# Two of three portions of each down projection as seven block products (Strassen's scheme)

## The chip, the cores and the metric

The kernel runs on one core of a Trainium2 chip. The metric is the device time of one execution in microseconds (us), as the median of repeated runs. The profile is one execution that the hardware profiler recorded; its engines are PE (TensorE), DVE (VectorE), ACT (ScalarE), POOL (GpSimd) and SP (SyncE, which issues the DMAs).

## The reference

Three layers on 512 tokens of 1024 features in float32: a sparse attention mixer and an FFN, a retention mixer and an FFN, a gated block with three branches and an FFN. The change touches the three FFNs alone, and of them the last product. One FFN is:

```python
def conv_ffn(h, w_up, conv_w, conv_b, w_down):
    seq = h.shape[1]
    u = h @ w_up
    up = jnp.pad(u, ((0, 0), (CONV_W - 1, 0), (0, 0)))
    u = sum(up[:, j:j + seq] * conv_w[j] for j in range(CONV_W)) + conv_b
    a, b = u[..., :D_FF], u[..., D_FF:]
    return (jax.nn.silu(a) * b) @ w_down
```

and the layer adds its result to `x`.

## The kernel before

**Layout and precision.** Activations stand with features on the 128 partitions and the 512 tokens along the free dimension: `X` holds 8 feature blocks of 128x512, `H` the normalised input. Each float32 product is made of three matmuls on rounded parts (`mm3`, lines 335 to 337): weight high part by activation high part, high by low, low by high. So each weight block (128x128) is loaded three times.

**Weights.** They come in units of up to 128x1024 (8 blocks for one output feature block), in one long order. SP loads a unit by DMA into one of four raw slots (`WS`, `load_to`, line 286). ACT rounds it to its high part (`WH`, `hi_to`, line 306), POOL takes the low part (`WL`, `lo_to`, line 316), three units at a time in `WH` and `WL`. A slot of `WH` is free when PE has used the unit three before. `hi_to` is called at fixed places of ACT's program, up to a unit counted from the one whose result ACT handles there (`P.ahead`).

**One FFN** has 22 pairs of up units (`up p` and `up 22+p`, 24 matmuls of 512 columns each) and three down portions over 8, 8 and 6 of the 22 inner feature blocks (`FFN_GROUPS`), each of 8 units with one output feature block. PE's order is ups 0 to 15, down 0, ups 16 to 21, down 1, down 2 (`pe_ffn`, line 578). For each up unit DVE multiplies the sum by the norm's row (line 664, "scaling"), ACT writes the third tap of the convolution (line 622, "tap") and DVE adds the two others (lines 666, 669). Then ACT takes the silu (line 626), DVE multiplies the halves (line 674), ACT rounds the product into `G` (line 632) and DVE takes its low part (line 677). For a down unit DVE adds the result to `X` (`dve_add_x`, line 571). At the start of an FFN the first scaling has to wait for the norm's row, so DVE and ACT begin some units behind PE.

Each engine executes its own fixed program; semaphores join them. Sums stand in eight PSUM banks (`ps`) of 128x512.

Two other places serve the prediction as measures: the gtg products of the gated block (line 335 on `G`, 16 groups of three matmuls of 256 columns) and the 64-row products of its attention (line 1863).

Of the kernel before, what the change touches and what calls it, by code (L numbers as in the profile page):

```python
# [16 lines left out]
T = 512  # L17
# [4 lines left out]
FFN_GROUPS = [(0, 8), (8, 16), (16, 22)]  # L22
RING = 3
STAGE = 4
# [4 lines left out]
def weight_units():  # L29
# [120 lines left out]
class Plan:  # L150


    def __init__(self, mem, dram, counted=None, sems=None):
        self.m, self.d, self.sems = mem, dram, sems
        self.count, self.value = {}, {}
        self.known = counted.value if counted else {}
        self.places = unit_places()[0]
        self.order = counted.order if counted else []
        self.index = counted.index if counted else {}
        self.unit_end = counted.unit_end if counted else {}  # L160
# [4 lines left out]
        self.hi_n = self.lo_n = self.in_n = 0  # L165
# [111 lines left out]

def load_to(P, e, n):

    while P.in_n < min(n, len(P.order)):  # L280
        i = P.in_n
        at, w = P.places[P.order[i]]
        if i >= STAGE:
            e.wait_ge(*P.at("w_lo", i - STAGE))
# [3 lines left out]
        P.in_n += 1  # L288


def w_parts(P, i):
    w = P.places[P.order[i]][1]
    s, f = i % RING * NXW, i % STAGE * NXW
    return P.m["WH"][:, s:s + w], P.m["WL"][:, s:s + w], P.m["WS"][:, f:f + w]


def hi_to(P, e, n):

    while P.hi_n < min(n, len(P.order)):
# [4 lines left out]
        if i >= RING:  # L304
            e.wait_ge(*P.at(*P.unit_end[i - RING]))
# [13 lines left out]
def unit(P, e, key, end):  # L319

    if key not in P.index:
        P.index[key] = len(P.order)
        P.order.append(key)
    if key not in P.begun:
        P.begun.add(key)
        e.wait_ge(*P.at("w_lo", P.index[key]))
    i = P.index[key]
    P.unit_end[i] = end
    w = P.places[key][1]
    s = i % RING * NXW  # L330
    return P.m["WH"][:, s:s + w], P.m["WL"][:, s:s + w]
# [245 lines left out]

def pe_ffn(P, e, L, ph):
    def up(g):
        for p in range(*FFN_GROUPS[g]):  # L580
            for m in (p, FT + p):
                feature(P, e, ("up", L, m), P.hs(), ready=(lambda k: [("h_lo", (ph, k))]) if m == 0 else None)
                if m == FT:
                    if L == 0:
                        e.wait_ge(*P.at("cr", "mean"))
                    row_mm(P, e, ph)

    def down(g):
        a, z = FFN_GROUPS[g]
        for m in range(8):  # L590
            feature(P, e, ("dn", L, g, m), [(P.G(p % 16 * T), P.G(8192 + p % 16 * T)) for p in range(a, z)],
                    ready=(lambda n: [("g_lo", (L, a + n))]) if m == 0 else None)
    up(0)
    up(1)
    down(0)
    up(2)
    down(1)
    down(2)


def act_ffn(P, e, L, ph, after, g_end, sc_end):
# [3 lines left out]
    def up(g):  # L605
        for p in range(*FFN_GROUPS[g]):
            s = 2 * (p % 2)
            for m, slot in ((p, s), (FT + p, s + 1)):
                key = ("up", L, m)
                if p == 0 and slot == 0:  # L610
                    e.preload_act_table_set("natural_log_exp_and_others")
                    act_row_split(P, e, ph, 7)
                    hi_to(P, e, P.ahead(("up", L, FT)))
                    act_row(P, e, ph)
                    hi_to(P, e, P.ahead(("up", L, 1), True))
                    e.wait_ge(*P.at("fp", L))
                    for ev in sc_end:
                        e.wait_ge(*P.at(*ev))
                if p >= 2:
                    e.wait_ge(*P.at(*(("silu", (L, p - 2)) if slot == s else ("mul", (L, p - 2)))))  # L620
                e.wait_ge(*P.at("f_u", key))
                e.activation(P.sc(slot * T), P.ps(key), ACT.Identity, bias=fp[:, 4 * m + 3:4 * m + 4],  # L622
                             scale=fp[:, 4 * m + 2:4 * m + 3]).then_inc(*P.sig("tap2", key))
                hi_to(P, e, P.ahead(key, True) + (1 if p in (1, 2, 3) else 0))
            e.wait_ge(*P.at("conv", ("up", L, p)))
            e.activation(P.ps(("up", L, p)), P.sc(s * T), ACT.Silu).then_inc(*P.sig("silu", (L, p)))
            e.wait_ge(*P.at("mul", (L, p)))
            if p == 0 and g_end:
# [5 lines left out]
    def down(g):
        for m in range(8):
            key = ("dn", L, g, m)
            hi_to(P, e, P.ahead(key))
            if after and g == 2:
                act_x(P, e, after, m, ("x", key))
    up(0)  # L640
    up(1)
    down(0)
    up(2)
    down(1)
    down(2)


def dve_ffn(P, e, L, ph, after, sc_end):
# [6 lines left out]
    def up(g):  # L655
        for p in range(*FFN_GROUPS[g]):
            s = 2 * (p % 2)
            for m, slot in ((p, s), (FT + p, s + 1)):
                key, c = ("up", L, m), P.sc(slot * T)
                u = P.ps(key)  # L660
                e.wait_ge(*P.at("feat", key))
                if m == 0:
                    e.wait_ge(*P.at("row", ph))
                e.tensor_tensor(u, u, P.m["ACC"][:, :], ALU.mult).then_inc(*P.sig("f_u", key))  # L664
                e.wait_ge(*P.at("tap2", key))
                e.scalar_tensor_tensor(c[:, 1:T], u[:, 0:T - 1], fp[:, 4 * m + 1:4 * m + 2], c[:, 1:T], ALU.mult,  # L666
                                       ALU.add).then_inc(*P.sig("tap1", key))
                e.wait_ge(*P.at("tap1", key))
                e.scalar_tensor_tensor(c[:, 2:T], u[:, 0:T - 2], fp[:, 4 * m:4 * m + 1], c[:, 2:T], ALU.mult,  # L669
                                       ALU.add).then_inc(*P.sig("conv", key))  # L670
            gate, g = P.ps(("up", L, p)), P.ps(("up", L, FT + p))
            e.wait_ge(*P.at("silu", (L, p)))
            e.wait_ge(*P.at("conv", ("up", L, FT + p)))
            e.tensor_tensor(g, gate, P.sc((s + 1) * T), ALU.mult).then_inc(*P.sig("mul", (L, p)))
            P.end["ps", ("up", L, p)] = ("mul", (L, p))
            e.wait_ge(*P.at("g_hi", (L, p)))
            e.tensor_tensor(P.G(8192 + p % 16 * T), g, P.G(p % 16 * T).bitcast(F), ALU.subtract).then_inc(
                *P.sig("g_lo", (L, p)))
            P.end["ps", ("up", L, FT + p)] = ("g_lo", (L, p))

    def down(g):
        for m in range(8):
            dve_add_x(P, e, ("dn", L, g, m), m, ("x", ("dn", L, g - 1, m)) if g else None)
            if after and g == 2 and m:
                dve_x(P, e, after, m - 1)
        if after and g == 2:
            dve_x(P, e, after, 7)
    up(0)
    up(1)
    down(0)  # L690
    up(2)
    down(1)
    down(2)


def pool_ffn(P, e, L):
    lo_to(P, e, P.ahead(("dn", L, 2, 7)))

# [1790 lines left out]
def act_program(P, e):  # L2489
# [12 lines left out]
    act_ret(P, e, "nf1", ("feat", ("dn", 0, 2, 7)))  # L2502
# [43 lines left out]
def sp_program(P, e):  # L2546
# [19 lines left out]
    weights(("dn", 0, 2, 6))  # L2566
# [10 lines left out]
    for m in range(8):  # L2577
        e.wait_ge(*P.at("x", ("dn", 1, 2, m)))
# [100 lines left out]
```

## Time and profile before

| | |
|---|---|
| median of three runs | 2140.15 us (2139.69 to 2142.06) |
| the profiled execution | 2140.16 us |
| its span (first to last instruction) | 2138.0 us |
| PE matmuls | 9723, busy 2122.6 us |
| granted TensorE clock | 1.0 over the span |
| DMA | 200.4 MB, mean 94 GB/s |

The span is what the trace covers; the execution's own time is 2.2 us longer. PE's busy time is the union of its matmuls, each of which overlaps the next: a 512-column matmul is shown with 390 ns and the next one starts 227 ns after it. The pace is therefore read from starts, not from durations. "Idle before" of an engine is time in which it waited, with the operation that ended the wait.

### The profile page before, as it was taken

Reading aid. Unit: us, or ns where it says so; the run is one execution under the profiler, and the core shown is the slowest. Engines: PE = TensorE matmul, PEld = TensorE weight load, DVE = VectorE, ACT = ScalarE, POOL = GpSimd, SP = SyncE. Lnnn points to the kernel's source line nnn. Section 1 sums busy time; section 2 is a strip of 40 time slices with the busy share of each in tenths; the row PEclk is TensorE's granted clock in tenths of the full one; section 3 lists DMA queues with packets and bytes.
Section 4 is the critical chain, followed back from the end, with each engine's and each line's share of the span. In section 5 each row is a group of like instructions: output and inputs, shape, how many; then the busy total and the mean of one; then the engine's idle time right before and its main releaser. Section 6 shows DMA issues by size and latency. Waiting matters only on the chain.

```text
span 2138.0 us, 25128 instructions
## 1 busy us (share of the span) xinstructions
PE 2122.6 (99%) x9723; PEld 1755.1 (82%) x9723; DVE 1094.9 (51%) x1756; ACT 931.5 (44%) x1378; POOL 924.6 (43%) x428
## 2 busy tenths in 40 slices
PE   9999999999999999999999999999999999999999
PEld 7868888888888888878888888888887888888887
DVE  7973555151634445475552424997577324553331
ACT  6564444242433424354442324445877434443331
POOL 3504444444434343434444444655432554444443
PEclk9999999999999999999999999999999999999999
DMA  4203232232322222222222224322222243223222
GB/s 165 70 11 103 97 98 93 87 109 92 121 84 89 84 99 74 98 73 97 94 94 101 96 87 167 107 80 79 70 70 70 95 134 99 98 94 102 91 94 84
DMA packets 57654, 200.41 MB, mean 94 GB/s; under 512 B 6400, under 2 KB 7168, under 8 KB 57280
## 3 DMA queue, kind: packets, MB, share of 16 engines
q1 hardware_dynamic: 56816, 197.46, 27.6%
q8 instruction: 78, 1.28, 0.3%
q10 hardware_dynamic: 720, 1.34, 0.2%
q14 instruction: 40, 0.33, 0.0%
HBM read 194.32 MB, written 4.19 MB: 93 GB/s over the span
## 4 chain that ended last, share of the span: by engine, by line
PE 96%; DVE 2%; issue 1%; ACT 1%; DMA 0%; ACTq 0%; DVEq 0%; POOL 0%
PE ps L335 29%; PE ps L337 28%; PE ps L336 28%; PE ps L365 2%; PE ps L363 2%; PE ps L364 2%; PE ps L1878 1%; PE ps L1271 1%; PE ps L1863 0%; PE ps L1890 0%; DMA X<-in_x 0%; PE ps L378 0%; PE ps L1865 0%; PE ps L1887 0%; DVE SC L2331 0%
## 5 line engine op out<-in xcount | busy, mean ns | idle before, releaser
L316 POOL TENSOR_TENSOR WL<-WS,WH 128x1024 fp32r<-128x1024 f32 (+1 forms) x360 | 853.1, 2371 | 1124.9 <-ACT WH L306 1124.6
L335 PE MATMUL ps<-H,WH 128*128 128x512 f32 (+2 forms) x1776 | 693.2, 390 | 2.8 <-DVE H L543 2.0
L337 PE MATMUL ps<-H,WL 128*128 128x512 f32 (+2 forms) x1776 | 690.5, 389 | 0.0
L336 PE MATMUL ps<-H,WH 128*128 128x512 f32 (+2 forms) x1776 | 690.5, 389 | 0.0
L306 ACT ACTIVATE WH<-WS 128x1024 fp32r<-128x1024 f32 (+2 forms) x362 | 374.8, 1037 | 432.5 <-PE ps L337 352.5
L335 PEld LDWEIGHTS ps<-H,WH 128*128 128x128 f32 (+1 forms) x1776 | 333.3, 188 | 73.8 <-DVE H L543 3.7
L337 PEld LDWEIGHTS ps<-H,WL 128*128 128x128 f32 (+1 forms) x1776 | 333.1, 188 | 69.1
L336 PEld LDWEIGHTS ps<-H,WH 128*128 128x128 f32 (+1 forms) x1776 | 333.4, 188 | 66.0
L335 PE MATMUL ps<-G,WH 128*128 128x512 f32 x880 | 343.2, 390 | 2.0 <-DVE G L1597 1.4
L337 PE MATMUL ps<-G,WL 128*128 128x512 f32 x880 | 342.8, 389 | 0.0
L336 PE MATMUL ps<-G,WH 128*128 128x512 f32 x880 | 342.8, 389 | 0.0
L571 DVE TENSOR_TENSOR X<-X,ps 128x512 f32<-128x512 f32 x120 | 81.7, 686 | 339.2 <-PE ps L337 338.4
L622 ACT ACTIVATE SC<-ps,FP 128x512 f32<-128x512 f32 x132 | 102.9, 779 | 334.4 <-DVE ps L664 334.4
L335 PEld LDWEIGHTS ps<-G,WH 128*128 128x128 f32 x880 | 165.3, 188 | 37.0 <-DVE G L1597 1.8
L337 PEld LDWEIGHTS ps<-G,WL 128*128 128x128 f32 x880 | 165.3, 188 | 34.4
L336 PEld LDWEIGHTS ps<-G,WH 128*128 128x128 f32 x880 | 165.3, 188 | 33.9
L666 DVE SCALAR_TENSOR_TENSOR SC<-ps,FP,SC 128x511 f32<-128x511 f32 x132 | 99.0, 750 | 125.8 <-ACT SC L622 125.8
L664 DVE TENSOR_TENSOR ps<-ps,ACC 128x512 f32<-128x512 f32 x132 | 92.1, 697 | 134.4 <-PE ps L337 128.1
L669 DVE SCALAR_TENSOR_TENSOR SC<-ps,FP,SC 128x510 f32<-128x510 f32 x132 | 98.9, 749 | 4.7
L2185 DVE SCALAR_TENSOR_TENSOR ps<-SC,PAR,ps 128x512 f32<-128x512 f32 x116 | 82.2, 754 | 1.9
L363 PE MATMUL ps<-WH,H 128*128 128x512 f32 x192 | 75.2, 392 | 0.0
L365 PE MATMUL ps<-WH,H 128*128 128x512 f32 x192 | 74.8, 389 | 0.0
(271 smaller groups left out, 1943.6 us busy)
## 6 DMA issues: line engine op xcount, KB each, us to landing
WS<-in_w SPq DMA_DIRECT2D x337, 512.0 KB, 3.2
WS<-in_w SPq DMA_DIRECT2D x24, 384.0 KB, 3.0
xs<-X SPq DMA_DIRECT2D x1, 2048.0 KB, 6.2
X<-xs SPq DMA_DIRECT2D x8, 256.0 KB, 4.0
out<-X SPq DMA_DIRECT2D x8, 256.0 KB, 2.0
X<-in_sg SPq DMA_DIRECT2D x1, 1344.0 KB, 5.6
X<-in_x ACTq DMA_DIRECT2D x4, 256.0 KB, 6.8
X<-in_x SPq DMA_DIRECT2D x4, 256.0 KB, 6.2
```

The source lines that it names most:

```text
L306: e.activation(hi, raw, ACT.Copy).then_inc(*P.sig("w_hi", i))
L316: e.tensor_tensor(lo, raw, hi.bitcast(F), ALU.subtract).then_inc(*P.sig("w_lo", i))
L335: e.matmul(out, lh, rh, start=start, stop=False)
L336: e.matmul(out, lh, rl, start=False, stop=False)
L337: return e.matmul(out, ll, rh, start=False, stop=stop)
L363: e.matmul(o, hh, wh[:, w], start=k == 0, stop=False)
L365: t = e.matmul(o, hl, wh[:, w], start=False, stop=k == 7)
L622: e.activation(P.sc(slot * T), P.ps(key), ACT.Identity, bias=fp[:, 4 * m + 3:4 * m + 4], scale=fp[:, 4 * m + 2:4 * m + 3]).then_inc(*P.sig ...
L664: e.tensor_tensor(u, u, P.m["ACC"][:, :], ALU.mult).then_inc(*P.sig("f_u", key))
L666: e.scalar_tensor_tensor(c[:, 1:T], u[:, 0:T - 1], fp[:, 4 * m + 1:4 * m + 2], c[:, 1:T], ALU.mult, ALU.add).then_inc(*P.sig("tap1", key))
L669: e.scalar_tensor_tensor(c[:, 2:T], u[:, 0:T - 2], fp[:, 4 * m:4 * m + 1], c[:, 2:T], ALU.mult, ALU.add).then_inc(*P.sig("conv", key))
L2185: e.scalar_tensor_tensor(c if j else P.sc(k * T), p[:, j:j + T], P.par("cvw", j * 4 + k), c, ALU.mult, ALU.add).then_inc(*P.sig("tap", (k, ...
```

## The change

The first two portions of each down projection (8 inner feature blocks each) are computed by Strassen's scheme in Winograd's form. For a pair `mp` of output feature blocks (m1, m2), the weights are split by even and odd inner blocks and by m1 and m2 into a11, a21, a12, a22, each four blocks of 128x128 side by side (128x512). The activations are split by even and odd blocks and by token halves, 256 columns each. In place of eight block products there are seven: a11, s1, s2, a12, s3, s4 and a22, where s1 = a21 + a22, s2 = s1 - a11, s3 = a11 - a21, s4 = a12 - s2. Each is 4 x 3 matmuls of 256 columns into half a PSUM bank, four pairs a portion.

- **PE** (`pe_down_pair`): the products in that order. a11, s2, s3 and a22 add onto one another in bank A, s1 and s4 in bank C, a12 has bank B. Between them DVE adds the state of the bank to a quarter of the pair's X, and PE waits for that before it goes on in the bank: s2 waits for the addition after a11, s3 for that after s2, a22 for that after s3, s4 for that after s1.
- **DVE**: the four weight sums of each pair from the raw slots into PSUM (`dve_sum`), their low parts (`dve_sum_lo`), and the seven additions of 256 columns (`dve_take`), in place of two of 512.
- **ACT**: the high parts of a11, a12, a22 and of the four sums (`act_form`). **POOL**: the low parts of a11, a12, a22 (`pool_raw_lo`). `WH` and `WL` are now six cells of 512, of which a unit takes two and a product one; a cell is free when PE has used what was there six cells before.
- **Activation forms**: the seven products need seven forms of the gated products, two of them plain. ACT and DVE make them while the up units run (`forms_1`, `forms_2`), for block p within the work on block p+1.
- **Order**: ups 0 to 9, first portion, ups 10 to 21, second portion, third portion. The convolution of the last up unit before a portion is put between the additions of its last pair.
- In `act_ffn` the call of `hi_to` for the first half reads `P.ahead(key, True)`, without one more for pairs 1 to 3.

The third portion keeps its form. The core of the diff:

```diff
-FFN_GROUPS = [(0, 8), (8, 16), (16, 22)]
+FFN_UPS = [(0, 10), (10, 22)]
...
+def pe_product(P, e, pair, name, low, o, form, first):
+
+    key = (pair, name)
+    cells(P, key, 1)
+    hi, lo = P.cell(key)
+    e.wait_ge(*P.at(low, key))
+    for q in range(4):
+        w = slice(128 * q, 128 * q + 128)
+        bh, bl = P.GX(4 * pair[1] + q, form, 0), P.GX(4 * pair[1] + q, form, 1)
+        e.matmul(o, hi[:, w], bh, start=first and q == 0, stop=False, skip_group_check=True)
+        e.matmul(o, hi[:, w], bl, start=False, stop=False, skip_group_check=True)
+        t = e.matmul(o, lo[:, w], bh, start=False, stop=q == 3, skip_group_check=True)
+    t.then_inc(*P.sig("prod", key))
...
+    a = own("A", seats["A", pair[2] % 2])
+    pe_product(P, e, pair, "a11", "w_lo", a, UP_B11, True)
+    c = own("C", seats["C"])
+    pe_product(P, e, pair, "s1", "fs_lo", c, UP_T1, True)
+    e.wait_ge(*P.at("x", (pair, "a11")))
+    pe_product(P, e, pair, "s2", "fs_lo", a, UP_T2, False)
+    b = own("B", seats["B"])
+    pe_product(P, e, pair, "a12", "w_lo", b, UP_B21, True)
+    e.wait_ge(*P.at("x", (pair, "s2")))
+    pe_product(P, e, pair, "s3", "fs_lo", a, UP_T3, False)
+    e.wait_ge(*P.at("x", (pair, "s1")))
+    pe_product(P, e, pair, "s4", "fs_lo", c, UP_B22, False)
+    e.wait_ge(*P.at("x", (pair, "s3")))
+    pe_product(P, e, pair, "a22", "w_lo", a, UP_T4, False)
...
-                hi_to(P, e, P.ahead(key, True) + (1 if p in (1, 2, 3) else 0))
...
+            tap2(p, s)
+            forms_1(p - 1)
+            if p < z - 1:
+                hi_to(P, e, P.ahead(("up", L, p), True))
+            forms_2(p - 1)
+            if p < z - 1:
+                tap2(FT + p, s + 1)
+                hi_to(P, e, P.ahead(("up", L, FT + p), True))
+                silu(p)
+                product(p)
+        for name in ("s2", "a12", "s3", "s4", "a22"):
+            act_form(P, e, (L, g, 0), name)
...
+    if name == "s1":
+        t = e.tensor_tensor(o, P.raw(pair, "a21"), P.raw(pair, "a22"), ALU.add)
...
+        t = e.tensor_tensor(o, P.ps((pair, "s1")), P.raw(pair, "a11"), ALU.subtract)
...
+        t = e.tensor_tensor(o, P.raw(pair, "a11"), P.raw(pair, "a21"), ALU.subtract)
...
+        t = e.tensor_tensor(o, P.raw(pair, "a12"), P.ps((pair, "s2")), ALU.subtract)
...
+def dve_take(P, e, pair, name, bank_name, m, half, before=None):
+
+    x = P.X(2 * pair[2] + m)[:, 256 * half:256 * half + 256]
+    e.wait_ge(*P.at("prod", (pair, name)))
+    e.tensor_tensor(x, x, P.ps((pair, bank_name))[:, 0:256], ALU.add).then_inc(*P.sig("x", (pair, name)))
```

The order on ACT at the start of an FFN, from the first silu on (line 626 before, 771 now), before:

```order
L626 ACTIVATE ps<-SC 128x512
L632 ACTIVATE G<-ps 128x512
L622 ACTIVATE SC<-ps,FP 128x512
L306 ACTIVATE WH<-WS 128x1024
L622 ACTIVATE SC<-ps,FP 128x512
L306 ACTIVATE WH<-WS 128x1024
L626 ACTIVATE ps<-SC 128x512
L632 ACTIVATE G<-ps 128x512
L622 ACTIVATE SC<-ps,FP 128x512
L306 ACTIVATE WH<-WS 128x1024
```

and now (765 is the tap, 361 the cast of a weight unit, 784, 786, 797 and 800 the activation forms):

```order
L771 ACTIVATE ps<-SC 128x512
L784 ACTIVATE SC<-ps 128x512
L765 ACTIVATE SC<-ps,FP 128x512
L797 ACTIVATE G_long<-ps 128x512
L765 ACTIVATE SC<-ps,FP 128x512
L361 ACTIVATE WH<-WS 128x1024
L771 ACTIVATE ps<-SC 128x512
L786 ACTIVATE G_long<-ps 128x512
L765 ACTIVATE SC<-ps,FP 128x512
L800 ACTIVATE G_long<-ps 128x256
L361 ACTIVATE WH<-WS 128x1024
```

The first cast (unit 6) stood behind the first tap of pair 1 and now stands behind the second; the next one (unit 7) stood behind that second tap and now stands behind the silu, a form, the first tap of pair 2 and another form.

The order on DVE in one settled pair of the first portion, from the addition after a11 on (line 888 is an addition to X, 878 a low part, 861, 866, 864 and 869 the next pair's sums s1, s3, s2 and s4); before, a down unit had one addition of 512 columns on DVE and nothing else there:

```order
L888 TENSOR_TENSOR X<-X,ps 128x256
L878 TENSOR_TENSOR WL<-ps,WH 128x512
L888 TENSOR_TENSOR X<-X,ps 128x256
L861 TENSOR_TENSOR ps<-WS 128x512
L888 TENSOR_TENSOR X<-X,ps 128x256
L866 TENSOR_TENSOR ps<-WS 128x512
L888 TENSOR_TENSOR X<-X,ps 128x256
L864 TENSOR_TENSOR ps<-ps,WS 128x512
L878 TENSOR_TENSOR WL<-ps,WH 128x512
L888 TENSOR_TENSOR X<-X,ps 128x256
L878 TENSOR_TENSOR WL<-ps,WH 128x512
L888 TENSOR_TENSOR X<-X,ps 128x256
```

The additions are those after a11, s1, s2, a12, s3 and s4; after this piece come the sum s4, the addition after a22 and the low part of s3, and the row of operations begins again. Every operation behind an addition waits on DVE until PE has ended that product.

## Rows read from the trace of the kernel before

**Rows 1.** The page, part 1: busy time, share of the span and instructions of each engine.

```profile
PE 2122.6 (99%) x9723; PEld 1755.1 (82%) x9723; DVE 1094.9 (51%) x1756; ACT 931.5 (44%) x1378; POOL 924.6 (43%) x428
```

**Rows 2.** The page, part 4: the chain that ended last, by engine, then by line.

```profile
PE 96%; DVE 2%; issue 1%; ACT 1%; DMA 0%; ACTq 0%; DVEq 0%; POOL 0%
PE ps L335 29%; PE ps L337 28%; PE ps L336 28%; PE ps L365 2%; PE ps L363 2%; PE ps L364 2%; PE ps L1878 1%; PE ps L1271 1%; PE ps L1863 0%; PE ps L1890 0%; DMA X<-in_x 0%; PE ps L378 0%; PE ps L1865 0%; PE ps L1887 0%; DVE SC L2331 0%
```

**Rows 3.** One down portion: us, busy (count) of PE, PEld, DVE, ACT, POOL; clock, DMA, GB/s.

```profile
1132.50:1176.02 43.52, 43.52 (x193) 36.05 (x192) 8.40 (x12) 10.25 (x11) 19.18 (x8) 1.00 0.30 101
```

**Rows 4.** Timeline of PE: start us, us, instruction; first and last of the 256-column row.

```profile
1388.68 0.28 PE L335 MATMUL ps<-G 128*128 128x256 f32 x1
...
1394.32 0.28 PE L337 MATMUL ps<-G 128*128 128x256 f32 x1
1394.44 0.40 PE L335 MATMUL ps<-H,WH 128*128 128x512 f32 x1
```

**Rows 5.** Timeline of PE and its weight loads (PEld) within that row.

```profile
1390.48 0.19 PEld L336 LDWEIGHTS ps<-G 128*128 128x128 f32 x1
1390.60 0.28 PE L336 MATMUL ps<-G 128*128 128x256 f32 x1
1390.60 0.19 PEld L337 LDWEIGHTS ps<-G 128*128 128x128 f32 x1
```

**Rows 6.** Timeline: a portion's last matmul and its addition; PE before the 64-row products.

```profile
1175.80 0.39 PE L337 MATMUL ps<-G,WL 128*128 128x512 f32 x1
1176.22 0.69 DVE L571 TENSOR_TENSOR X<-X,ps 128x512 f32<-128x512 f32 x1 [4.75 <-PE ps L337]
...
1501.92 0.39 PE L337 MATMUL ps<-H,WL 128*128 128x512 f32 x1
1502.24 0.44 PE L1863 MATMUL ps<-G 64*128 64x128 f32 x4
```

**Rows 7.** Groups by form: busy us, mean ns of one, idle before.

```profile
L664 DVE TENSOR_TENSOR ps<-ps,ACC 128x512 f32<-128x512 f32 x132 | 92.1, 697 | 134.4 <-PE ps L337 128.1
L2254 DVE TENSOR_TENSOR TMP<-ps,X 64x256 f32<-64x256 f32 x16 | 6.8, 422 | 3.3 <-PE ps L337 2.8
L632 ACT ACTIVATE G<-ps 128x512 fp32r<-128x512 f32 x66 | 39.5, 599 | 62.5 <-DVE ps L674 62.5
L2465 POOL TENSOR_TENSOR G<-X,G 128x512 fp32r<-128x512 f32 x8 | 10.3, 1294 | 6.0 <-ACT G L2146 5.7
```

**Rows 8.** Timeline of DVE, ACT, POOL and PE where the second FFN starts.

```profile
981.67 0.70 DVE L674 TENSOR_TENSOR ps<-ps,SC 128x512 f32<-128x512 f32 x1 [0.38 <-ACT ps L626]
983.04 0.69 DVE L677 TENSOR_TENSOR G<-ps,G 128x512 fp32r<-128x512 f32 x1 [0.67 <-ACT G L632]
983.64 0.69 DVE L664 TENSOR_TENSOR ps<-ps,ACC 128x512 f32<-128x512 f32 x1
...
984.37 0.78 ACT L622 ACTIVATE SC<-ps,FP 128x512 f32<-128x512 f32 x1 [1.36 <-DVE ps L664]
985.05 1.05 ACT L306 ACTIVATE WH<-WS 128x1024 fp32r<-128x1024 f32 x1
988.04 1.05 ACT L306 ACTIVATE WH<-WS 128x1024 fp32r<-128x1024 f32 x1
...
989.16 2.40 POOL L316 TENSOR_TENSOR WL<-WS,WH 128x1024 fp32r<-128x1024 f32 x1 [0.58 <-ACT WH L306]
...
991.06 0.39 PE L335 MATMUL ps<-H,WH 128*128 128x512 f32 x1
...
996.50 0.39 PE L335 MATMUL ps<-H,WH 128*128 128x512 f32 x1
```

**Rows 9.** Timeline of DVE and POOL in the retention mixer, from 570 us.

```profile
570.18 2.95 POOL L316 TENSOR_TENSOR WL<-WS,WH 128x1024 fp32r<-128x1024 f32 x1 [1.85 <-ACT WH L306]
570.18 0.68 DVE L902 TENSOR_TENSOR SC<-SC 128x512 f32<-128x512 f32 x1
570.78 2.90 DVE L904 TENSOR_TENSOR SC<-SC 128x512 f32<-128x512 f32 x1
```

More of the change, by code:

```diff
@@ L21 @@
 FT = 22
[L22 removed]
+FFN_UPS = [(0, 10), (10, 22)]
 RING = 3
+CELL = 512
+CELLS = 6
 STAGE = 4
@@ L275, in drop, with seat, raw_ends @@
     P.free.append(P.slot["ps", key])
+def seat(P, key, b):
+    P.before[key] = P.user.get(("ps", b))
+    P.user["ps", b] = key
+    P.slot["ps", key] = b
+    return P.m["banks"][b]
+def raw_ends(P, i):
+    key = P.order[i]
+    if key[0] != "dns":
+        return [("w_lo", i)]
+    pair, second = key[1:4], key[4]
+    return [("w_lo", (pair, "a22")), ("fs", (pair, "s4"))] if second else [("w_lo", (pair, "a11")), ("fs", (pair, "s2"))]
 def load_to(P, e, n):
@@ L316, in lo_to, with listed @@
         e.tensor_tensor(lo, raw, hi.bitcast(F), ALU.subtract).then_inc(*P.sig("w_lo", i))
-def unit(P, e, key, end):
+def listed(P, key):
     if key not in P.index:
@@ L572, in dve_add_x @@
     P.end["ps", key] = ("x", key)
-def pe_ffn(P, e, L, ph):
[L579 to L598, printed above, removed]
+UP_B11, UP_T1, UP_B21, UP_B22, UP_T3, UP_T4, UP_T2 = range(7)
@@ L634, in down, with tap2 @@
[L634 to L645, printed above, removed]
+    def tap2(m, slot):
+        key, p = ("up", L, m), m % FT
+        if p >= 2:
+            e.wait_ge(*P.at(*(("silu", (L, p - 2)) if m < FT else ("mul", (L, p - 2)))))
+        e.wait_ge(*P.at("f_u", key))
+        e.activation(P.sc(slot * T), P.ps(key), ACT.Identity, bias=fp[:, 4 * m + 3:4 * m + 4],
+                     scale=fp[:, 4 * m + 2:4 * m + 3]).then_inc(*P.sig("tap2", key))
@@ L653, in dve_ffn @@
     dve_row(P, e, ph, P.m["ACC"][:, :])
-    def up(g):
-        for p in range(*FFN_GROUPS[g]):
-            s = 2 * (p % 2)
[L658 to L693, printed above, removed]
-def pool_ffn(P, e, L):
-    lo_to(P, e, P.ahead(("dn", L, 2, 7)))
+    def scale(m):
+        key = ("up", L, m)
+        u = P.ps(key)
+        e.wait_ge(*P.at("feat", key))
+        if m == 0:
+            e.wait_ge(*P.at("row", ph))
+        e.tensor_tensor(u, u, P.m["ACC"][:, :], ALU.mult).then_inc(*P.sig("f_u", key))
@@ new lines, in dve_ffn, with pool_raw_lo @@
+    for m in range(8):
+        dve_add_x(P, e, ("dn", L, m), m, ("x", ((L, 1, m // 2), "a22")))
+        if after and m:
+            dve_x(P, e, after, m - 1)
+    if after:
+        dve_x(P, e, after, 7)
+def pool_raw_lo(P, e, pair, name):
+    key = (pair, name)
+    hi, lo = P.cell(key)
+    e.wait_ge(*P.at("w_hi", key))
+    e.tensor_tensor(lo, P.raw(pair, name), hi.bitcast(F), ALU.subtract).then_inc(*P.sig("w_lo", key))
+def pool_ffn(P, e, L):
+    for g, (a, z) in enumerate(FFN_UPS):
+        lo_to(P, e, P.ahead(("up", L, FT + z - 1)))
+        for mp in range(4):
+            for name in ("a11", "a12", "a22"):
+                pool_raw_lo(P, e, (L, g, mp), name)
+        P.lo_n = P.index.get(("dns", L, g, 3, 1), 0) + 1
+    lo_to(P, e, P.ahead(("dn", L, 7)))
```

353 lines of the change are left out of this document (305 added, 48 removed).

## Prediction, made before the change was run

> **What bounds the kernel now.** I read four views, in this order. The page says that PE is busy for 2122.6 of 2138.0 us [rows 1], and the chain that ended last is 96% PE, nearly all of it in the three matmul lines 335 to 337 [rows 2]. DVE, ACT and POOL are busy for about half of the span, so their work costs nothing until PE waits for one of them. The third view is one down portion by itself (the first of the second FFN): 192 matmuls of 512 columns take the whole of a stretch of 43.52 us, so 226.7 ns each, at full granted clock, with DVE busy for only 8.4 us of it and POOL for 19.2 [rows 3]. PE never pauses there. A change of such a portion is therefore worth what PE's own time changes, less any new wait. The fourth view is the only long row of 256-column matmuls in the program (the gtg products, every one with its own weight load): 48 of them from 1388.68 until the next matmul starts at 1394.44, 5.76 us, so 120.0 ns each [rows 4].
>
> **PE's work in the six changed portions** (two in each of three layers). Before: 8 units x 24 matmuls = 192 x 226.7 ns = 43.52 us [rows 3]. Now: 4 pairs x 7 products x 4 x 3 = 336 matmuls of half the width, at 120.0 ns [rows 4], 40.32 us. The gain is 3.20 us a portion, **19.2 us** for six. Half the columns do not halve the time: a 512 takes 226.7 and two 256 take 240, so of the 12.5% that seven products instead of eight save, 5.9% is given back. The third portion of each layer keeps its 8 x 18 matmuls.
>
> Would the weight load, of which there are now 336 instead of 192, cost more than that? In [rows 5] a load of 190 ns starts with every matmul and the next starts 120 ns later: loads overlap matmuls and one another. The Trainium skill (TensorE: Matmul & The Clock Gate, section on the mechanism of tile packing) says that LDWEIGHTS overlaps matmuls in flight only when the row group differs; all loads here use all rows, so by that rule load and matmul would add up. The trace does not agree, and I keep the 120.0.
>
> **Handovers between products.** Each product begins with one or two waits on PE. A wait that is already met costs nothing at the end of the 256 row (120 ns to the next unit's first matmul, [rows 4]). The other bound is a break of about 0.1 us, as PE shows where it goes on to the 64-row products (1501.92 to 1502.24, 0.32 us from start to start against 0.227 [rows 6]); 168 products x 0.093 = 15.6 us. Below zero there is nothing, as PE has no pauses to lose in a portion. I take zero, since [rows 4] are the same form of matmul with the same kind of signals, and keep 15.6 for the range.
>
> **What DVE, ACT and POOL must do in a pair of 10.08 us** (7 x 12 x 120 ns). DVE gets four sums and four low parts of 512 columns (0.69 us each, 0.61 from start to start when nothing is waited for) and seven additions of 256 columns (0.42) [rows 7, 8]: 7.8 to 8.5 us of 10.08. ACT gets seven casts of 0.60 to 0.63 us, 4.3; POOL three low parts of 1.30, 3.9 [rows 7]. All three fit, DVE only just. What counts is when three of DVE's additions end, because PE adds the next product onto the same bank: a11's before s2 starts (2.88 us into the pair), s2's before s3 (5.76), s3's before a22 (8.64). I laid DVE's rows in the order that the second excerpt above shows from these durations. A product that ends for PE at t shows its result at t + 0.2 us (the last matmul starts at t - 0.12 and lasts 0.28 [rows 4]; DVE follows PE's end by 0.03, as where the portion's last matmul starts at 1175.80 and its addition at 1176.22 [rows 6]). DVE's timetable of a settled pair is then: a22 of the pair before 0.20 to 0.62, low part s3 to 1.23, **a11 1.64 to 2.06**, low part s4 to 2.67, s1 3.08 to 3.50, the next pair's sum s1 to 4.2, **s2 4.52 to 4.94**, next sum s3 to 6.0, a12 to 6.4, next sum s2 to 7.0, its low part s1 to 7.6, **s3 7.55 to 7.97**, low part s2 to 8.6, s4 8.84 to 9.26, next sum s4 to 9.87. The three additions end 0.7 to 0.8 us early. This holds with a lock that the trace shows: a DVE operation with both inputs in SBUF that meets a running POOL operation waits for it (line 904 takes 2.90 us instead of 0.69, and POOL's is drawn out from 2.4 to 2.95 by the one before) [rows 9]. Two of the sums (s1, s3) read only SBUF. In the timetable POOL's low parts run from 2.35 (a22), from 4.15 (next a11) and from 8.4 (a12), so that the sum s1 waits about 0.2 us and the sum s3 about 0.6; both are in the times just given. So a settled pair costs no wait.
>
> The **first pair** of a portion is tighter, because DVE comes from the convolution of the last feature block, and in the first portion of a layer from the forms of block 8 too. By the same durations the first portion goes so: block 9's scaling starts at -5.24, its tap on ACT only at -4.30 (two casts are ahead of it), its taps on DVE end at -1.95, block 8's low part at -1.35; then come five sums and low parts to 1.9, low part s3 to 2.5, and the addition after a11 ends at 2.87 against 2.88. The late sums meet POOL at 3.8 and 5.5, wait 0.8 and 0.9 us, and the addition after s3 ends at 8.95 against 8.64. I put 0.4 us on each first portion and 0.1 on each second: **+1.5 us**. Bounds: nothing, and 1.3 us (one more POOL operation in the way) in each of six, 7.8.
>
> **The start of each layer's FFN.** Here DVE and ACT begin late, as they wait for the norm's row, and catch up over some units. The change moves the cast of unit 6 (the up units counted from 0) behind ACT's second tap, drops the early cast for pairs 1 to 3, and puts new forms between (first excerpt). Before, unit 6 was cast at 985.05 and unit 7 at 988.04, its low part was done at 991.56, and PE came to them at 991.06 and 996.50 [rows 8]. Laid out anew from 981.67 with the same durations: unit 6 cast at 987.34, low part done at 990.86, 0.2 us ahead of PE; unit 7 cast at 993.35, done at 996.85, 0.35 behind, and some 0.1 more until PE runs again; unit 8 is level, and unit 9 is 0.7 us ahead. That is 0.5 us in each of three layers, **+1.5 us**. Elsewhere the forms cost nothing: for every two blocks DVE gets 3.2 us more (two of its low parts were there before; now three, one of 256 columns and five sums of 256) and ACT at most 1.8, beside 21.8 us of PE's matmuls (96 x 226.7 ns), of which DVE is then busy for 14.8. Only if that cover were gone would they count, 24 x 3.2 = 77 us. Bounds: nothing, and 1.5 us in each layer.
>
> Loads cost nothing: two units of 512 KB in 10.08 us instead of one in 5.44, 102 against 94 KB a us, with the engines at 30% [rows 3], and a pair's slots come free some 10 us ahead of use. **The sum**: 2140.16 (the profiled execution, 0.01 above the median) - 19.2 + 1.5 + 1.5 = **2124.0 us**.
>
> **The rivals.**
> 1. *DVE late in every pair, yet not the bound.* For it: margins of 0.7 us built on handovers of 0.04 to 0.1 us, over fifteen DVE operations and two locks. Against: 1.6 us a pair are idle. At 0.4 us a pair, 24 pairs lose 9.6: 2133 us. Chance 0.17.
> 2. *A break at each product*, as bounded above, 15.6 us less the waits it hides: 2136 to 2140, no difference. Chance 0.08.
> 3. *DVE becomes the bound of the pairs, and the change loses.* Place: the strict order of additions and sums. If no operation overlaps the one before (8.5 us), each takes a handover of 0.08 (1.2) and both SBUF sums wait for a whole POOL operation (2.6), a pair lasts 12.3 us, and 24 pairs cost 53 us more: 2176. It decides from 10.88 us a pair (43.52 / 4): above it the change is a loss. For it: DVE's 84% in the pairs, the most of any engine but PE; against it: the lock hits only a sum that meets a POOL operation, POOL runs 39% of a pair, and it would have to do so every time. Chance 0.12.
> 4. *Loads not overlapped at half width.* 256 columns stream in 107 ns (226.7 - 120.0, the step from 256 to 512 columns), and with a load of 190 ns behind each that is 297 ns x 336, 99.8 us a portion, six times 56.3 us more than now: 2479. [Rows 5] speak against it, and so do [rows 3], where a 512 would then take 403 ns and takes 226.7; chance 0.01. The skill's rule named above would make this case.
>
> **How the numbers follow.** Forecast 0.62: 2124.0, between 2121 (no wait anywhere) and 2129. Rival 1 fills 2129 to 2136. About 4.3 us (0.2%) is what a measurement of this kernel tells from no change, so "faster" ends at 2135.9: forecast and rival 1, with a little of rival 2, give 0.80; same 0.08; slower 0.12. A range of 2120 to 2137 leaves out rival 3, half of rival 2 and little else.
>
> **What would show it.** Right: 2016 matmuls of 128x256 at the product's three lines with 120 ns from start to start, portions of 40.3 to 41.5 us; about half a us lost at unit 7 of each layer; no wait at a settled pair's s2, s3 and a22. Rival 1: PE idle before those, released by DVE's additions, 0.2 to 0.5 us each. Rival 2: steps of over 200 ns at each product's first matmul, with the additions long done. Rival 3: DVE over 95% busy in the pairs. Wrong altogether: another step than 120 ns within a product, or waits in a part that the change leaves alone.

## The result, and the profile after

| | before | after |
|---|---|---|
| median of the runs | 2140.14 us (2139.69 to 2142.06, 4 runs) | 2128.45 us (2127.71 to 2128.54, 4 runs) |
| the profiled execution | 2140.16 us | 2127.71 us |
| its span | 2138.0 us | 2125.9 us |

The ratio is 0.9943, with a 95% interval of 0.9926 to 0.996. The change is worth 11.7 us, where 16.1 were forecast (2124.0). The page of the changed kernel, part 1, and the chain that ended last, by engine; they answer to [rows 1] and [rows 2]:

```profile
PE 2107.9 (99%) x10587; PEld 1779.9 (84%) x10587; DVE 1318.7 (62%) x2236; ACT 1017.3 (48%) x1570; POOL 907.7 (43%) x452
...
PE 90%; DVE 5%; ACT 2%; issue 1%; DMA 0%; POOL 0%; SPq 0%; ACTq 0%; DVEq 0%
```

PE is still the bound, with 864 more matmuls and 14.7 us less of busy time. DVE is now in the chain with 5%, ACT with 2%. Where, the stretches tell. Of the changed kernel, each stretch with the busy time (count) of PE, PEld, DVE, ACT and POOL, then clock, DMA share and GB/s: a settled pair of the first portion, the second portion of the first layer, the first portion of the second. [Rows 3] are the portion before.

```profile
318.42:328.50 10.08, 10.08 (x87) 10.08 (x86) 8.23 (x15) 4.18 (x7) 4.14 (x3) 1.00 0.34 109
...
479.23:520.86 41.63, 40.80 (x337) 40.41 (x336) 35.06 (x63) 18.58 (x31) 17.21 (x13) 1.00 0.31 99
1063.76:1104.37 40.61, 40.57 (x338) 40.37 (x336) 34.04 (x62) 19.01 (x31) 17.57 (x12) 1.00 0.33 107
```

A settled pair takes 84 x 120.0 ns = 10.08 us and PE does not pause in it; DVE is busy for 8.2 us of that. A first portion takes 40.61 us, a second one 41.63, against 43.52 before. So the two kinds differ by a whole microsecond, and the prediction had them the other way round (40.7 and 40.4). The groups by line and form, of the changed kernel (line, engine, operation, count | busy, mean ns of one | idle before, releasers):

```profile
L666 PE MATMUL ps<-G_long,WH 128*128 128x256 f32 x672 | 191.0, 284 | 2.6 <-DVE X L888 1.6 <-DVE WL L878 0.9
L866 DVE TENSOR_TENSOR ps<-WS 128x512 f32<-128x512 f32 x24 | 26.1, 1087 | 0.0
L861 DVE TENSOR_TENSOR ps<-WS 128x512 f32<-128x512 f32 x24 | 25.4, 1059 | 0.0
```

The products' first line waited for additions to X (line 888), and for a sum's low part (line 878), which the prediction had not named. The two sums that read only SBUF (lines 861 and 866) took 1059 and 1087 ns on average, not 690: the lock of [rows 9].

**The second portion's start**, DVE and POOL of the changed kernel before 479.23, where the portion begins (timeline: start us, us, engine line operation [idle before <- releaser]); line 928 is the low part of block 20, 861 the sum s1, 1039 the low part of a11 (released by its cast on ACT, line 753), 905 the scaling of the last up unit:

```profile
473.73 0.69 DVE L928 TENSOR_TENSOR G<-ps,G 128x512 fp32r<-128x512 f32 x1 [0.66 <-ACT G L780]
474.29 1.29 POOL L1039 TENSOR_TENSOR WL<-WS,WH 128x512 fp32r<-128x512 f32 x1 [5.86 <-ACT WH L753]
474.33 1.81 DVE L861 TENSOR_TENSOR ps<-WS 128x512 f32<-128x512 f32 x1
476.06 0.69 DVE L905 TENSOR_TENSOR ps<-ps,ACC 128x512 f32<-128x512 f32 x1
```

The same place ahead of the first portion, which begins at 308.04:

```profile
302.40 0.69 DVE L861 TENSOR_TENSOR ps<-WS 128x512 f32<-128x512 f32 x1
303.00 0.69 DVE L905 TENSOR_TENSOR ps<-ps,ACC 128x512 f32<-128x512 f32 x1
...
303.72 1.29 POOL L1039 TENSOR_TENSOR WL<-WS,WH 128x512 fp32r<-128x512 f32 x1 [6.20 <-ACT WH L753]
```

In the first portion the sum s1 runs before POOL's low part of a11 and takes 0.69 us; the last scaling starts 5.04 us ahead of the portion. In the second, DVE first waits 0.66 us for block 20's cast and takes its low part; by then POOL has started a11, 0.04 us ahead of the sum, and the sum takes 1.81 us. The last scaling starts only 3.17 us ahead. What it does to PE, in the second portion (timeline of PE):

```profile
480.54 0.28 PE L668 MATMUL ps<-G_long,WL 128*128 128x256 f32 x1
481.13 0.36 PE L666 MATMUL ps<-G_long,WH 128*128 128x256 f32 x1 [0.31 <-DVE WL L878]
481.32 0.28 PE L667 MATMUL ps<-G_long,WH 128*128 128x256 f32 x1
...
482.52 0.28 PE L668 MATMUL ps<-G_long,WL 128*128 128x256 f32 x1
483.32 0.39 PE L666 MATMUL ps<-G_long,WH 128*128 128x256 f32 x1 [0.53 <-DVE X L888]
483.55 0.28 PE L667 MATMUL ps<-G_long,WH 128*128 128x256 f32 x1
```

Read from starts, over the pace of 120 ns: 0.47 + 0.07 us at the product s1, 0.69 + 0.10 at s2, together 1.3 us. The small second parts are the step after the waiting matmul, 190 and 220 ns instead of 120. The other two second portions show the same within 0.02 us. A first portion has one wait, before s2, 0.19 + 0.10 us (the step after it is again 0.22; the addition after a11 ends at 311.05):

```profile
310.79 0.28 PE L668 MATMUL ps<-G_long,WL 128*128 128x256 f32 x1
311.10 0.39 PE L666 MATMUL ps<-G_long,WH 128*128 128x256 f32 x1
```

**The start of an FFN**, POOL and PE of the changed kernel in the second layer (line 371 is a unit's low part, 393 to 395 the up matmuls); it answers to the POOL and PE lines of [rows 8]:

```profile
984.31 2.40 POOL L371 TENSOR_TENSOR WL<-WS,WH 128x1024 fp32r<-128x1024 f32 x1 [10.13 <-ACT WH L361]
...
986.47 0.39 PE L395 MATMUL ps<-H,WL 128*128 128x512 f32 x1
986.86 0.47 PE L393 MATMUL ps<-H,WH 128*128 128x512 f32 x1
...
990.36 2.39 POOL L371 TENSOR_TENSOR WL<-WS,WH 128x1024 fp32r<-128x1024 f32 x1 [3.64 <-ACT WH L361]
992.16 0.39 PE L395 MATMUL ps<-H,WL 128*128 128x512 f32 x1
992.90 0.47 PE L393 MATMUL ps<-H,WH 128*128 128x512 f32 x1 [0.35 <-POOL WL L371]
993.20 0.39 PE L394 MATMUL ps<-H,WH 128*128 128x512 f32 x1
```

Unit 6 is 0.16 us late (986.47 to 986.86 is 0.39, less 0.227) and unit 7 0.51 (0.74 less 0.227), with 0.08 more behind each: 0.83 us a layer. Both start 0.15 us after POOL's end.

**The sum of what the trace shows**: 2140.16 - 19.2 (PE's own work) + 3 x 0.3 (first portions) + 3 x 1.3 (second portions) + 3 x 0.83 (FFN starts) = 2128.3, against 2127.71 for the profiled execution and 2128.45 for the median. The two profiled executions differ by 0.5 us in a part that the change leaves alone: a step of PE of 1.80 us in the first mixer, the same in both, begins at 158.34 us before and at 157.81 after. With it the sum is met within 0.1 us.

### The profile page after: what moved, and what is told of

The parts are those of the page before. It is cut to its first block, busy times and chain, and to the rows that moved or that the text cites. A ratio compares the mean times of both kernels' runs of the same rounds, so it can differ in the third digit from the quotient of the medians.

```text
span 2125.9 us, 27915 instructions
## 1 busy us (share of the span) xinstructions
PE 2107.9 (99%) x10587; PEld 1779.9 (84%) x10587; DVE 1318.7 (62%) x2236; ACT 1017.3 (48%) x1570; POOL 907.7 (43%) x452
## 4 chain that ended last, share of the span: by engine, by line
PE 90%; DVE 5%; ACT 2%; issue 1%; DMA 0%; POOL 0%; SPq 0%; ACTq 0%; DVEq 0%
PE ps L393 23%; PE ps L395 23%; PE ps L394 23%; PE ps L666 4%; PE ps L667 4%; PE ps L668 4%; PE ps L423 2%; PE ps L422 2%; PE ps L421 2%; ACT SC L765 1%; DVE SC L910 1%; PE ps L2229 1%; DVE SC L916 1%; PE ps L1622 1%; PE ps L2214 0%
## 5 line engine op out<-in xcount | busy, mean ns | idle before, releaser
L371 POOL TENSOR_TENSOR WL<-WS,WH 128x1024 fp32r<-128x1024 f32 (+1 forms) x312 | 738.1, 2368 | 956.2 <-ACT WH L361 956.0
L361 ACT ACTIVATE WH<-WS 128x1024 fp32r<-128x1024 f32 (+2 forms) x314 | 324.7, 1035 | 248.0 <-PE ps L395 164.4
L393 PE MATMUL ps<-G,WH 128*128 128x512 f32 x496 | 193.6, 390 | 2.0 <-DVE G L1948 1.4
L666 PE MATMUL ps<-G_long,WH 128*128 128x256 f32 x672 | 191.0, 284 | 2.6 <-DVE X L888 1.6
L394 PE MATMUL ps<-G,WH 128*128 128x512 f32 x496 | 193.1, 389 | 0.0
L395 PE MATMUL ps<-G,WL 128*128 128x512 f32 x496 | 193.1, 389 | 0.0
L667 PE MATMUL ps<-G_long,WH 128*128 128x256 f32 x672 | 190.1, 283 | 0.0
L668 PE MATMUL ps<-G_long,WL 128*128 128x256 f32 x672 | 190.1, 283 | 0.0
L1039 POOL TENSOR_TENSOR WL<-WS,WH 128x512 fp32r<-128x512 f32 x72 | 98.7, 1374 | 173.7 <-ACT WH L753 171.9
L629 DVE TENSOR_TENSOR X<-X,ps 128x512 f32<-128x512 f32 x72 | 48.7, 685 | 139.7 <-PE ps L395 139.7
L666 PEld LDWEIGHTS ps<-G_long,WH 128*128 128x128 f32 x672 | 128.9, 192 | 4.6 <-DVE X L888 2.9
L667 PEld LDWEIGHTS ps<-G_long,WH 128*128 128x128 f32 x672 | 128.9, 192 | 0.2
L668 PEld LDWEIGHTS ps<-G_long,WL 128*128 128x128 f32 x672 | 128.9, 192 | 0.0
```

The lines of the kernel that those rows point to most:

```text
L361: e.activation(hi, raw, ACT.Copy).then_inc(*P.sig("w_hi", i))
L371: e.tensor_tensor(lo, raw, hi.bitcast(F), ALU.subtract).then_inc(*P.sig("w_lo", i))
L393: e.matmul(out, lh, rh, start=start, stop=False)
L394: e.matmul(out, lh, rl, start=False, stop=False)
L395: return e.matmul(out, ll, rh, start=False, stop=stop)
L666: e.matmul(o, hi[:, w], bh, start=first and q == 0, stop=False, skip_group_check=True)
```

## The experiments

Theory A says: the second portions lose 1.3 us each by what stands ahead of them on DVE, the low part of block 20 and the lock behind it, and the rest of the pair is sound. Its rivals are that the waits come from the chain of casts and cells on ACT and POOL (e1_s1_first), and that the sum is long for another reason than the lock (e2_a11_later); for the starts of the FFNs the rival is that the new forms hold the casts back by themselves (e3_early_cast). Each expectation says what they would give. The interval of each ratio is against runs of the kernel before, made beside it.

**e1_s1_first: the sum s1 ahead of block 20's low part, in second portions.**

```diff
-            if p == z - 1:
+            if p == z - 1 and g == 0:
                 dve_sum(P, e, (L, g, 0), "s1")
...
                 mul(p)
+                if g == 1 and p == z - 2:
+                    dve_sum(P, e, (L, g, 0), "s1")
                 forms_0(p)
```

Expected:

> Against the changed kernel (2128.45 us). In each second portion DVE's sum s1 is issued ahead of block 20's low part, in the time in which DVE waits for ACT there. Theory A (the waits of the second portions, 0.46 + 0.69 us and a little of refilling, come from DVE reaching the last scaling 1.9 us later than in the first portions, through the low part and the lock with POOL on the sum s1): the scaling starts 1.7 us earlier, the sum s1 takes 0.69 instead of 1.81 us, both waits of each second portion go or fall below 0.3 us, portions of 41.6 us become 40.3 to 40.6; all in all 3.0 to 3.9 us less, about 2125. Theory B (the waits come from the chain of casts and cells on ACT and POOL, which is not moved): the two waits stay, 41.6 us a portion, 2128.4.

Measured: 2124.15 us (2123.91 to 2126.39), ratio 0.9922 (0.9907 to 0.9937), 4.3 us less than the change by the medians, a little more than the 3.0 to 3.9 expected; the spans of the two profiled executions differ by 3.8 (2122.1 against 2125.9). DVE ahead of the second portion, and the whole portion (columns as above):

```profile
473.02 0.69 DVE L861 TENSOR_TENSOR ps<-WS 128x512 f32<-128x512 f32 x1
473.77 0.69 DVE L928 TENSOR_TENSOR G<-ps,G 128x512 fp32r<-128x512 f32 x1
474.38 0.69 DVE L905 TENSOR_TENSOR ps<-ps,ACC 128x512 f32<-128x512 f32 x1
...
479.28:519.59 40.31, 40.31 (x337) 40.31 (x336) 33.27 (x61) 18.20 (x31) 17.22 (x13) 1.00 0.32 102
```

The sum fills the 0.66 us in which DVE had waited for ACT, takes 0.69 us, and the last scaling starts 4.90 us ahead of the portion. The portion has no wait left: 40.31 us, which is 336 x 120.0 ns. Theory A holds, and the rival is out, since nothing was changed on ACT and POOL; the same matmuls with the same handovers lose nothing once DVE is in time.

**e2_a11_later: only the lock taken away, in second portions.** ACT casts s1 before a11, so that POOL starts a11's low part later.

```diff
-                act_form(P, e, (L, g, 0), "a11")
-                act_form(P, e, (L, g, 0), "s1")
+                for name in (("a11", "s1") if g == 0 else ("s1", "a11")):
+                    act_form(P, e, (L, g, 0), name)
```

Expected:

> Against the changed kernel (2128.45 us). In each second portion ACT casts the sum s1 before a11, so that POOL takes a11's low part only after the sum s1: the lock alone is removed, the low part of block 20 stays ahead of the sum. Theory A (lock and order together): sum s1 0.69 instead of 1.81 us, the scaling 1.1 us earlier, the first wait (0.46 us before product s1) gone, of the second (0.69 before s2) at most 0.3 left: 2.4 to 3.9 us less in all, 2124.6 to 2126. If the lock were not the cause (the sum long for another reason, as a late load of the weights): the sum stays at 1.8 us and the time at 2128.4.

Measured: 2126.35 us (2125.75 to 2127.83), ratio 0.9931 (0.9916 to 0.9946), 2.1 us less than the change, where at least 2.4 were expected. The sum s1 on DVE, POOL's low part of a11, which now comes well behind it, then PE at its one wait:

```profile
475.08 0.69 DVE L861 TENSOR_TENSOR ps<-WS 128x512 f32<-128x512 f32 x1
...
477.00 1.29 POOL L1039 TENSOR_TENSOR WL<-WS,WH 128x512 fp32r<-128x512 f32 x1 [7.82 <-ACT WH L753]
...
482.73 0.28 PE L668 MATMUL ps<-G_long,WL 128*128 128x256 f32 x1
483.31 0.39 PE L666 MATMUL ps<-G_long,WH 128*128 128x256 f32 x1 [0.29 <-DVE X L888]
483.53 0.28 PE L667 MATMUL ps<-G_long,WH 128*128 128x256 f32 x1
```

The sum takes 0.69 us again, the wait before the product s1 is gone, and the portion takes 40.87 us. The expectation had at most 0.3 us left at s2; 0.46 + 0.10 are left. So of the 1.3 us the lock is 0.76, and what is left, 0.56, is the order (block 20's low part and the wait for its cast, ahead of the sum), since e1_s1_first takes it away as well. The theory had given the lock too much.

**e3_early_cast: the early cast of pairs 1 to 3 restored.**

```diff
-                hi_to(P, e, P.ahead(("up", L, p), True))
+                hi_to(P, e, P.ahead(("up", L, p), True) + (1 if p in (1, 2, 3) else 0))
...
-                hi_to(P, e, P.ahead(("up", L, FT + p), True))
+                hi_to(P, e, P.ahead(("up", L, FT + p), True) + (1 if p in (1, 2, 3) else 0))
```

Expected:

> Against the changed kernel (2128.45 us). Pairs 1 to 3 of each FFN cast one unit further ahead again, as in the kernel before; the forms stay. Theory: the two waits at units 6 and 7 of each FFN (0.25 and 0.6 us with refilling) come from the later casts; they go, 2.4 to 2.6 us less, 2125.9. Rival: the added forms on ACT and DVE hold the casts back by themselves, so that half or more of the 0.85 us in each FFN stays, 2127 to 2128.4.

Measured: 2125.84 us (2125.61 to 2127.42), ratio 0.9929 (0.9915 to 0.9944), 2.6 us less than the change. POOL at the start of the second FFN:

```profile
982.57 2.40 POOL L371 TENSOR_TENSOR WL<-WS,WH 128x1024 fp32r<-128x1024 f32 x1 [7.05 <-ACT WH L361]
985.66 2.41 POOL L371 TENSOR_TENSOR WL<-WS,WH 128x1024 fp32r<-128x1024 f32 x1 [0.70 <-ACT WH L361]
```

The low parts of units 6 and 7 now follow each other within 3.1 us, where in the change they stood 6.05 apart, and PE waits for neither in any layer. The activation forms that stand between the casts cost nothing there. So the loss at the start was the dropped "+ 1", and not the new forms.

**e4_all: the version that beats both.** e1 and e3 together, and in the first pair of a portion the addition after a11 ahead of the low part of s3:

```diff
-            dve_sum_lo(P, e, pair, "s3")
+            if mp:
+                dve_sum_lo(P, e, pair, "s3")
             dve_take(P, e, pair, "a11", "A", 0, 0)
+            if mp == 0:
+                dve_sum_lo(P, e, pair, "s3")
```

Expected:

> Sum s1 first in the second portions, early casts in pairs 1 to 3, and in the first pair of each portion the addition after a11 before the low part of s3. If the three causes are right and add up, PE has no wait in the FFNs: 7.4 us less than the changed kernel with its waits (0.9 of them in the first portions), 2120.5 to 2121.5, and all six portions last 40.3 us. If one wait only hid another, 2122 or more.

Measured: 2121.34 us (2120.94 to 2121.53), ratio 0.9907 (0.989 to 0.9924): 18.8 us less than the kernel before (2140.14), 7.1 less than the change. The time is as expected; that no wait would be left is not. The two kinds of portion, then DVE at the sums of the first pair and PE where it still waits, all in the first layer:

```profile
307.03:347.61 40.58, 40.58 (x338) 40.37 (x337) 34.06 (x62) 18.93 (x31) 17.57 (x12) 1.00 0.34 108
478.19:518.51 40.32, 40.32 (x338) 40.31 (x337) 33.22 (x61) 18.18 (x31) 17.25 (x13) 1.00 0.33 101
...
310.90 1.32 DVE L861 TENSOR_TENSOR ps<-WS 128x512 f32<-128x512 f32 x1
312.46 1.46 DVE L866 TENSOR_TENSOR ps<-WS 128x512 f32<-128x512 f32 x1
...
315.55 0.28 PE L668 MATMUL ps<-G_long,WL 128*128 128x256 f32 x1
315.83 0.39 PE L666 MATMUL ps<-G_long,WH 128*128 128x256 f32 x1
316.05 0.28 PE L667 MATMUL ps<-G_long,WH 128*128 128x256 f32 x1
```

The wait before s2 is gone from the first portions, but DVE has no pause between 305.88 and 316.6 and the two sums lose 0.63 and 0.77 us to the lock. The lateness comes out at a22 instead, 0.16 + 0.10 us. Of the first portion's 0.3 us only 0.03 was won (40.58 us for 40.61). That the locks are what is left there is argued and not shown: taking them away in the first portions was not tried.

**e5_split: the price of half width and the weight load by themselves.** The kernel before, with each 512-column matmul of the first two down portions cut into two of 256 columns, each with its own weight load: 384 a portion, and nothing else is changed in number, size or order. It does not compute the sums right (both halves begin a sum in the same bank; that this is the reason no run shows), and serves for the time alone.

```diff
...
+        first, last = n == 0, n == len(rows) - 1
+        for c in (slice(0, 256), slice(256, 512)):
+            e.matmul(o[:, c], wh[:, w], rh[:, c], start=first, stop=False, skip_group_check=True)
+            e.matmul(o[:, c], wh[:, w], rl[:, c], start=False, stop=False, skip_group_check=True)
+            t = e.matmul(o[:, c], wl[:, w], rh[:, c], start=False, stop=last, skip_group_check=True)
```

Expected:

> Against the kernel before (2140.14 us). Its first two down portions with each matmul of 512 columns in two of 256, each with its own weight load, the same sums otherwise. If a 256-column matmul costs 120.0 ns in a long row of real work and a handover nothing: 6 x 192 x (240.0 - 226.7) ns = 15.4 us more, 2155.5, portions of 46.1 us. If halving cost nothing (the load hidden, 113.3 ns each): 2140. If loads did not overlap at half width: over 2250.

Measured: 2156.0 us (2155.07 to 2157.8) against 2140.41 for the kernel before, ratio 1.0073 (1.0058 to 1.0088). The first layer's first portion (the second takes 46.07 too):

```profile
375.02:421.09 46.07, 46.07 (x386) 46.07 (x384) 8.40 (x12) 10.25 (x11) 19.16 (x8) 1.00 0.30 97
```

46.07 / 384 = 120.0 ns, where the other engines have little to do. It costs 2.55 us a portion, 15.3 in six, and 15.6 were measured. That is the price of the half width with the number of products unchanged; seven eighths of 46.08 is the 40.32 of the prediction. The row also shows the weight loads (PEld) busy for the whole stretch beside the matmuls. The Trainium skill (TensorE: Matmul & The Clock Gate, the mechanism of tile packing) says that a load overlaps matmuls in flight only when the row group differs, though the same section lets PE pull a load into the background weight buffer ahead. The trace disagrees with the first with 384 loads of all rows in a row, and does not tell whether the second is what happens.

**e6_more1 and e7_more3: how much room DVE has.** In the changed kernel one more DVE operation of 512 columns (a sum into a scratch tile that nobody reads) behind the addition after s2 of every pair; then three. The excerpt is that of three; with one it reads `range(1)`.

```diff
             dve_take(P, e, pair, "s2", "A", 0, 1)
+            for i in range(3):
+                if i == 2:
+                    e.wait_ge(*P.at("more", (pair, 0)))
+                e.tensor_tensor(P.TMP(i % 2), P.ps((pair, "s3")), P.m["ACC"][:, :], ALU.add).then_inc(*P.sig("more", (pair, i)))
+                P.end["ps", (pair, "s3")] = ("more", (pair, i))
```

Expected of one:

> Against the changed kernel (2128.45 us). One more DVE operation of 512 columns (PSUM and ACC into an unused tile) in every pair, behind the addition after s2. Theory (DVE has 1.8 us a pair to spare and 0.7 us before each wait, part of it given back because the sum s3 then meets no lock): no wait in the settled pairs, at most 0.5 us in each first pair: 2128.4 to 2131.5. Rival (DVE is as good as the bound): 0.6 us in each of 24 pairs, 2143.

Expected of three:

> As the run before, with three more operations in every pair: DVE's 8.2 us of 10.08 become 10.1, and the addition after s3 would end at 9.2 us of the pair against 8.64. Theory: every pair now waits, 0.5 to 1.2 us, 24 pairs: 2140 to 2157, the first loss against the kernel before at about 0.5 us a pair. If PE did not depend on DVE's additions: 2128.4.

Measured: one more 2128.63 us (2128.53 to 2129.42), ratio 0.9945 (0.9929 to 0.9962), no different from the change; three more 2146.04 us (2145.56 to 2146.72), ratio 1.0025 (1.0015 to 1.0035), slower than the kernel before by 5.6 us. A settled pair with one more (columns as above):

```profile
329.13:339.21 10.08, 10.08 (x86) 10.08 (x85) 8.42 (x16) 4.18 (x7) 4.16 (x3) 1.00 0.32 106
```

One with three more, and of its timeline the added operations, the sum s3 and PE's first matmul of a22, which the addition after s3 releases:

```profile
318.90:329.80 10.90, 10.32 (x85) 10.12 (x85) 9.52 (x19) 4.06 (x9) 4.14 (x3) 1.00 0.30 97
...
325.18 1.88 DVE L1008 TENSOR_TENSOR TMP<-ps,ACC 128x512 f32<-128x512 f32 x3
327.10 0.70 DVE L866 TENSOR_TENSOR ps<-WS 128x512 f32<-128x512 f32 x1
...
329.70 0.39 PE L666 MATMUL ps<-G_long,WH 128*128 128x256 f32 x1 [0.58 <-DVE X L888]
```

With one more the pair stays at 10.08 us. With three PE waits 0.74 + 0.10 us before a22 in the middle pairs (1.00 + 0.10 in a portion's first, 0.12 + 0.10 in its last, less than the 0.5 that was expected of every pair), and a pair takes 10.9 us, 43.52 / 4 = 10.88: the point from which rival 3 was to decide. The portions (43.6 and, with the loss of the second ones, 44.6 us) no longer gain, and the waits at portion and FFN starts are left over as the loss. One operation more adds only 0.19 us of busy time to the pair, 8.42 for 8.23, because in its place the sum s3 comes after POOL's low part and no longer waits for it (0.70 us with one as with three, where it took 1.10 in the change).

## Why the prediction was right, and where it missed

- **PE's own work, -19.2 us: right.** The step is 120.0 ns within the products and from one to the next; portions without a wait take 40.31 us (e1_s1_first) for 40.32. e5_split shows the price of the half width apart from the scheme.
- **Weight loads overlapped: right**, by e5_split; rival 4 is out.
- **Handovers between products, 0: right.** No step over 120 ns in a settled pair with the additions in time; rival 2 (15.6 us) is out. A wait that is not met costs its length and 0.07 to 0.10 us more.
- **A settled pair costs no wait: right.** DVE's additions in the settled pair that begins at 318.42, the two sums, and POOL's low parts of a22 and a11 in one line (timeline, changed kernel):

```profile
320.04 0.42 DVE L888 TENSOR_TENSOR X<-X,ps 128x256 f32<-128x256 f32 x1 [0.42 <-PE ps L668]
...
320.81 2.99 POOL L1039 TENSOR_TENSOR WL<-WS,WH 128x512 fp32r<-128x512 f32 x2 [2.45 <-ACT WH L753]
...
321.82 0.84 DVE L861 TENSOR_TENSOR ps<-WS 128x512 f32<-128x512 f32 x1
322.92 0.42 DVE L888 TENSOR_TENSOR X<-X,ps 128x256 f32<-128x256 f32 x1 [0.26 <-PE ps L668]
323.26 1.10 DVE L866 TENSOR_TENSOR ps<-WS 128x512 f32<-128x512 f32 x1
...
325.90 0.41 DVE L888 TENSOR_TENSOR X<-X,ps 128x256 f32<-128x256 f32 x1
```

  Those after a11, s2 and s3 end at 2.04, 4.92 and 7.89 us of the pair; 2.06, 4.94 and 7.97 were laid out. The sum s1 waited 0.15 us for POOL and the sum s3 0.41, for 0.2 and 0.6. Rival 1 did not come about. Rival 3 has the right mechanism and the right point, but its condition is more than one operation of 512 columns away and less than about three.
- **The first pair of a portion, +1.5: the step that failed.** For the first portions it put 0.4 us and 0.3 was measured, so the size is close, but in part by luck: the wait is at s2 alone (the addition after a11 ends at 3.01 us of the portion for 2.87 laid out) and not at a22, where it had DVE late by 0.31 (the addition after s3 ends at 8.72 for 8.95, as the two sums lose 0.62 and 0.77 us to the lock for 0.8 and 0.9, and PE is 0.3 late itself). For the second it put 0.1, and 1.3 was measured, 3.9 us in all for 0.3: within the bound of 7.8, but it is nearly the whole miss. The prediction laid the first portion out row by row and took the second to be looser because it has no forms of block 8. It did not lay out what stands there in their place: block 20 is a plain block, whose low part DVE takes behind a wait for ACT's cast and ahead of the sum s1. That puts the sum just behind POOL's start on a11. e1_s1_first undoes it, e2_a11_later parts it into lock (0.76) and order (0.56).
- **The start of each FFN, +1.5: right in kind, under-sized.** 0.83 us a layer were measured for 0.5, 2.5 in all; e3_early_cast gives 2.6 back. Unit 6 was to be 0.2 us in time and was 0.16 late. The timetable ran to the end of POOL's low part and left out the handover: PE starts 0.15 us after it, at both units. The other 0.2 is the cast itself: laid out to start 3.72 us before PE comes to unit 6, it started 3.51 before (983.19 in the change's timeline, against 986.47 + 0.23).
- **The convolution's forms at nothing elsewhere: right**; in e3_early_cast no wait is left in an FFN outside the down portions.

The miss, 4.4 us, is then 3.6 from the second portions and 1.0 from the starts, less 0.3 from the first portions, 4.3 in all. The range (2120 to 2137) held the time since the bounds of these same terms were in it.

## What to carry to other kernels

When a change has the same structure at two places, lay out both from the order of the instructions: the place that looks easier may have one operation more ahead of its first critical one. And run a timetable to where the waiting engine starts, not to where the releasing one ends: here 0.15 us of handover and some 0.1 us of restart were as large as the margins that the table showed. Here the order on the fullest engine but PE counted around the change of stage and not in the settled pairs, and an operation put into a stretch in which that engine waited for another was free (e1_s1_first).

## What the hardware showed that was not expected

- **What the lock costs goes by when POOL ends.** The sum s1 started 0.04 us after POOL's low part of a11 (474.33 against 474.29) and took 1.81 us; 1.3 us before it, it took 0.69. In the Trainium skill (SBUF — State Buffer, the section on the two separate sides) the pair of ports that DVE, with two inputs in SBUF, shares with GpSimd is held for the whole instruction by whoever starts first. The trace agrees: every sum that meets a running POOL operation ends 0.56 us behind POOL's end, in the settled pair (323.80 and 324.36), in the first pairs and here (475.58 and 476.14). What a sum would have taken 0.05 us earlier, just ahead of POOL, no run shows.
- **A wait of PE has a tail.** After each one, the matmul that waited and the next are 190 to 220 ns apart instead of 120 (256 columns), and some 0.08 us are lost at 512 columns. With a wait of 0.2 us it is a third of the cost.
- **More work for DVE can cost less than its own time.** One more operation a pair added 0.19 us to DVE's busy time instead of 0.6, as it moved the sum behind it out of the lock.
